# Splits, norm and queue order around the block turns of a three-product FFN phase

## The reference

```python
def conv_ffn(h, conv_hist, w_up, w_dw, b_dw, w_down):
    up = h @ w_up                                   # 1024 -> 2*2816
    ext = jnp.concatenate([conv_hist, up], axis=1)
    c = ext[:, 0:T] * w_dw[0] + ext[:, 1:T + 1] * w_dw[1] + ext[:, 2:T + 2] * w_dw[2] + b_dw
    a, b = jnp.split(c, 2, axis=-1)
    return (jax.nn.silu(a) * b) @ w_down, ext[:, -(CONV_W - 1):]
...
ffn, new_conv = conv_ffn(x1, conv_hist, w_up, w_dw, b_dw, w_down)
ple = jax.nn.sigmoid(x1 @ w_pg) * (pe @ w_pe)
x2 = layer_norm(ALPHA * x1 + ffn + ple, ln2_g, ln2_b)
```

## Time and profile before

| | |
|---|---|
| time, median of 3 runs | 3105.6 us (3100.81 to 3105.85) |
| profiled execution, own time | 3105.37 us |
| its span | 3103.6 us |
| busy in the span: PE, DVE, ACT, POOL | 92%, 68%, 47%, 41% |
| FFN phase in the span | 1444 to 3104 us |

### The profile page before, as it was taken

How to read it: one execution, slowest core, us unless ns; L and a number is a source line. 1 busy time by engine, 2 the same in 40 slices (tenths; PEclk the granted TensorE clock), 3 DMA queues, 4 the chain that set the end, 5 groups by cost and what they waited for, 6 DMA issues and landing times. The chain is left out here.

```text
span 3103.6 us, 47421 instructions
## 1 busy us (share of the span) xinstructions
PE 2870.4 (92%) x14597; PEld 2481.3 (80%) x14597; DVE 2119.3 (68%) x2977; ACT 1458.5 (47%) x2959; POOL 1265.7 (41%) x932
## 2 busy tenths in 40 slices
PE   8998998999998899998799999779999987899996
PEld 6877786777776788887788888768999986788885
DVE  5635677877776444445678777776787779677776
ACT  4333556777876222214335444433454454355553
POOL 5332645766766433334243333342222225222223
PEclk9997998999999999999999999899999998999998
DMA  4226451222233333325533232542333343333331
GB/s 134 85 81 138 147 162 41 56 51 43 42 90 125 111 101 101 109 99 181 163 101 110 95 132 101 163 137 87 112 105 97 102 158 117 114 115 118 113 106 53
DMA packets 234858, 333.26 MB, mean 107 GB/s; under 512 B 66896, under 2 KB 109616, under 8 KB 233360
## 3 DMA queue, kind: packets, MB, share of 16 engines
q1 hardware_dynamic: 234736, 331.76, 34.9%
HBM read 246.05 MB, written 85.63 MB: 107 GB/s over the span
## 5 line engine op out<-in xcount | busy, mean ns | idle before, releaser
L3059 DVE TENSOR_TENSOR mx_w_lo<-ff_w_raw,mx_w_hi 128x512 fp32r<-128x512 f32 x302 | 287.7, 957 | 14.3 <-ACT mx_w_hi L2873 14.3
L3116 DVE TENSOR_TENSOR ho_raw<-ho_raw,ff_d 128x512 f32<-128x512 f32 x264 | 169.3, 682 | 139.1 <-PE ff_d L86 117.9
L1567 POOL TENSOR_TENSOR at_p_lo<-at_p,at_p_hi 128x512 fp32r<-128x512 f32 (+2 forms) x160 | 188.7, 1180 | 162.9 <-ACT at_p_hi L1604 161.0
L2769 POOL TENSOR_TENSOR mx_odd<-ff_d_raw,mx_odd 128x512 fp32r<-128x512 f32 x66 | 101.5, 1537 | 375.9 <-ACT mx_odd L2882 375.7
L2873 ACT ACTIVATE mx_w_hi<-ff_w_raw 128x512 fp32r<-128x512 f32 x390 | 229.4, 622 | 31.9 <-POOL ff_w_raw L2757 29.6
L2882 ACT ACTIVATE mx_odd<-ff_d_raw 128x512 fp32r<-128x512 f32 x66 | 41.3, 626 | 418.9 <-PE ff_d L86 401.7
L1597 ACT ACTIVATE at_p<-at_s 128x512 f32<-128x512 f32 (+1 forms) x320 | 170.4, 533 | 109.2 <-PE at_s L1793 56.2
L1709 DVE TENSOR_TENSOR at_p_lo<-at_p,at_p_hi 128x512 fp32r<-128x512 f32 (+1 forms) x160 | 189.0, 1182 | 43.1 <-ACT at_p_hi L1604 42.2
L2733 POOL TENSOR_TENSOR mx_w_lo<-ff_w_raw,mx_w_hi 128x512 fp32r<-128x512 f32 x88 | 121.3, 1378 | 224.2 <-ACT mx_w_hi L2873 224.2
L3092 DVE SCALAR_TENSOR_TENSOR ff_cv_a<-ff_up_a,ff_taps,ff_cv_a 128x768 f32<-128x768 f32 (+1 forms) x132 | 163.3, 1237 | 61.1 <-ACT ff_cv_a L2939 33.3
L84 PE MATMUL ff_d<-mx_odd,ff_h_hi 128*128 128x512 f32 x364 | 148.7, 409 | 42.1 <-DVE ho_raw L3116 19.9
(11 more groups left out here) (556 smaller groups left out, 9980.9 us busy)
## 6 DMA issues: line engine op xcount, KB each, us to landing
ff_w_raw<-in_w_ffn_p SPq DMA_DIRECT2D x216, 256.0 KB, 3.3
ff_w_raw<-scratch_sums SPq DMA_DIRECT2D x176, 256.0 KB, 2.7
ff_d_raw<-in_w_ffn_p SPq DMA_DIRECT2D x132, 256.0 KB, 2.8
scratch_sums<-ff_w_raw SPq DMA_DIRECT2D x84, 256.0 KB, 3.7
ho_raw<-in_x SPq DMA_DIRECT2D x17, 512.0 KB, 4.3
mx_m_raw<-scratch_mix_t SPq DMA_DIRECT2D x17, 512.0 KB, 5.2
scratch_x_t<-mx_work SPq DMA_DIRECT2D x17, 512.0 KB, 2.6
scratch_y<-mx_work SPq DMA_DIRECT2D x17, 512.0 KB, 2.9
```

What stands on the lines that cost most here:

```text
L1567: pool.tensor_tensor(p_lo[:, e % H_RING, 0:b - a], p[:, e % P_RING, 0:b - a], f32(p_hi[:, e % H_RING, 0:b - a]), ALU.subtract).then_inc(lo ...
L2769: pool.tensor_tensor(lo, d_raw[:, :], f32(hi), ALU.subtract).then_inc(dlo, 1)
L3059: dve.tensor_tensor(w[j][1], raw, f32(w[j][0]), ALU.subtract).then_inc(wlo_dve, 1)
L3116: dve.tensor_tensor(y[t][:, H[i]], y[t][:, H[i]], ps_d[2 * (t % 2) + i][:, :], ALU.add)\
```

## The change

- Token lows T1 and T4 of blocks 1 and 2 are made on DVE instead of POOL. On ACT, T2's high moves from the end of a block to the beginning of the next.
- The norm of blocks 0 and 1 is two DVE instructions per tile (`normalise`: subtract mean and times gain; times 1/sigma and plus bias) and the power on POOL (`root`), in periods 0 and 1 of the next block, instead of four steps on three engines. The norm of block 2, at the end of the kernel, stays.
- ACT does copies 1 and 2 ahead of the down highs and of the weight and token highs that stood before them; down highs 1 and 3 move from ahead of `product_hi` to behind copy 1, down high 2 behind copy 2 and S2's high.
- DVE does `hidden_low` and join 0 right behind S4's low, ahead of the lows of A22, A11 and A12. In even periods S1's low stands ahead of the first add instead of behind it.
- SP issues the loads of y one by one through the periods: in block 0 through period 1, later through periods 1 and 2, each store of a tile ahead of its load.

The core of the diff:

```diff
-POOL_X = (T1, T4)
-DVE_X = (B11, B21, T2, T3, B22)
+POOL_X = ((T1, T4), (), ())
+DVE_X = tuple(tuple(j for j in range(PRODUCTS) if j not in POOL_X[b]) for b in range(3))
...
@@ SP
             def even_loads(b, f, p, at_next, at_d, turning=False):
+                if turning:
+                    load_y(b, 3)
+                    if BLOCKS[b] > 4:
+                        load_y(b, 4)
+                    for t in range(5, BLOCKS[b - 1]):
+                        store_y(b - 1, t)
+                    for t in range(5, BLOCKS[b]):
+                        load_y(b, t)
                 next_loads(b, f, p, 0, at_next, () if b == 0 else (A11, A22))
                 load_down(b, p, at_d, 0)
-                if turning:
-                    for t in (2, 3):
-                        load_y(b, t)
...
-                    if turning and j in (4, 5):
-                        for t in (2 * j - 8, 2 * j - 7):
-                            store_y(b - 1, t)
-                if turning:
-                    for t in (0, 1):
-                        load_y(b, t)
+                    if turning and b == 0 and j > 0:
+                        load_y(0, j - 1)
+                    if turning and b > 0 and 0 < j < 6:
+                        store_y(b - 1, j - 1)
+                        if j > 2:
+                            load_y(b, j - 3)
...
-                    for t in range(BLOCKS[0]):
-                        load_y(0, t)
-                odd_loads(b, 1, 0, 3, (-1, 12), turning=b > 0)
+                odd_loads(b, 1, 0, 3, (-1, 12), turning=True)
@@ POOL
+            def root(b, tiles):
+                for t in tiles:
+                    pool.wait_ge(eps, FIRST[b] + t + 1)
+                    pool.tensor_tensor(rstd[:, t:t + 1], var_eps[:, t:t + 1], power[:, :], ALU.pow).then_inc(rs, 1)
...
                     down_lows(b - 1, LAST, (3,))
-                    tokens(b, POOL_X)
-                    offsets(b - 1, range(BLOCKS[b - 1]))
-                    scale(b - 1, range(0, 4))
+                    root(b - 1, range(BLOCKS[b - 1]))
                     even(b, 0, 0)
-                    down_lows(b, 0, (1,))
-                    scale(b - 1, (4,))
-                    down_lows(b, 0, (2,))
-                    scale(b - 1, (5,))
-                    weight_low(b, 2, S3)
-                    weight_low(b, 2, S4)
+                    odd(b, 1, 0)
@@ ACT, period
+                if begins and b > 0:
+                    tokens(b, (T2,))
                 copy(b, f, i, 0)
...
-                if i == 1:
-                    down_highs(b, p, (0, 1) if at_end(b, p) else (1,))
-                elif before is not None:
-                    down_highs(before[0], before[2], (3,))
+                if at_end(b, p) and i == 1:
+                    down_highs(b, p, (0,))
                 if more:
                     weights(nb, nf, (A11,))
                 carry_in(b, f, p, i, 1)
                 if before is not None:
                     product_hi(*before[:4])
+                if begins and b > 0:
+                    tokens(b, (T3,))
+                copy(b, f, i, 1)
+                if i == 1:
+                    down_highs(b, p, (1,))
+                elif before is not None:
+                    down_highs(before[0], before[2], (3,))
                 if more:
                     weights(nb, nf, (A12,))
                 if begins:
-                    tokens(b, (T3, B22, T4) if b else (B22, T4))
-                copy(b, f, i, 1)
+                    tokens(b, (B22, T4))
                 if x_next:
                     tokens(b + 1, (B11,))
-                if centring is not None:
-                    centre(b - 1, centring[0])
-                if i == 1:
-                    down_highs(b, p, (2,))
                 copy(b, f, i, 2)
                 if more:
                     weights(nb, nf, (S2,))
+                if i == 1:
+                    down_highs(b, p, (2,))
@@ DVE
+            def normalise(b, tiles):
+                dve.wait_ge(ln_in, 32)
+                for t in tiles:
+                    n = FIRST[b] + t + 1
+                    dve.scalar_tensor_tensor(y[t], y[t], neg_mean[:, t:t + 1], ln_g[:, :], ALU.add, ALU.mult)\
+                       .then_inc(gained, 1)
+                    dve.wait_ge(rs, n)
+                    dve.wait_ge(gained, n)
+                    dve.scalar_tensor_tensor(y[t], y[t], rstd[:, t:t + 1], ln_b[:, :], ALU.mult, ALU.add)\
+                       .then_inc(shifted, 1)
...
                     convolve(*before, 0)
+                    if begins:
+                        tokens(b, (T2,))
                     convolve(*before, 1)
                     gate(*before)
-                    weights(b, f, (S4, A22), par)
...
+                    weights(b, f, (S4,), par)
+                    hidden_low(*before)
+                    join(b, f, par, 0)
+                    weights(b, f, (A22,), par)
+                    if begins:
+                        tokens(b, (T1,))
+                    weights(nb, nf, (A11, A12) if more else ())
...
+                        if t == 3:
+                            tokens(b, (T4,))
                 join(b, f, par, 1)
...
                 if more:
                     weights(nb, nf, (S2,))
+                if norm[1]:
+                    normalise(b - 1, norm[1])
                 if par == 0:
+                    weights(nb, nf, (S1,) if more else ())
                     if adds is not None and isinstance(adds[1], int) and adds[1] == 0:
                         dve.wait_ge(y_in, 16 * (FIRST[b] + BLOCKS[b]))
                     if adds is not None:
                         add(*adds, 0)
-                    weights(nb, nf, (S1,))
-                    if adds is not None:
                         add(*adds, 1)
...
-                period(b, 0, 0, (b - 1, FT - 1, LAST, 1) if b else None, after_last=b > 0)
+                period(b, 0, 0, (b - 1, FT - 1, LAST, 1) if b else None, after_last=b > 0,
+                       norm=((), (), (0, 1)) if b else none)
                 dve.wait_ge(const_in, 16)
-                period(b, 1, 1, (b, 0, 0, 0), shifts=((), (), (0, 1), (2, 3)) if b else none)
-                period(b, 2, 0, (b, 1, 0, 1), adds=(b, 0), shifts=((4,), (5,), (), ()) if b else none)
+                period(b, 1, 1, (b, 0, 0, 0), norm=((2,), (3,), (4, 5)) if b else none)
+                period(b, 2, 0, (b, 1, 0, 1), adds=(b, 0))
```

More of the change, by code:

```diff
@@ L2780, in offsets @@
                 for t in tiles:
[L2781 to L2784, removed]
+                    root(b, (t,))
+                    pool.wait_ge(rs, FIRST[b] + t + 1)
                     pool.tensor_tensor(offset[:, t:t + 1], neg_mean[:, t:t + 1], rstd[:, t:t + 1], ALU.mult)\
@@ L2789, in scale @@
                 for t in tiles:
[L2790 removed]
+                    pool.wait_ge(centred, t + 1)
                     pool.tensor_tensor(y[t], y[t], ln_g[:, :], ALU.mult).then_inc(scaled, 1)
@@ L2971, in centre, with period @@
                 for t in tiles:
-                    act.wait_ge(offs, FIRST[b] + t + 1)
+                    act.wait_ge(offs, t + 1)
                     act.activation(y[t], y[t], ACT.Identity, scale=rstd[:, t:t + 1],
                                    bias=offset[:, t:t + 1]).then_inc(centred, 1)
-            def period(b, f, p, i, before, x_next=False, centring=None):
+            def period(b, f, p, i, before, x_next=False):
                 nb, nf = following(b, f, 1)
@@ L3016, in period @@
                     weights(nb, nf, (S1, S3))
-                if x_next:
-                    tokens(b + 1, (T2,))
-                if centring is not None:
-                    centre(b - 1, centring[1])
                 if i == 0 and not at_end(b, p):
@@ L3025, in _ @@
             for b in range(3):
-                period(b, 0, 0, 0, (b - 1, FT - 1, LAST, 1, 1) if b else None, centring=((0, 1), (2, 3)) if b else None)
+                period(b, 0, 0, 0, (b - 1, FT - 1, LAST, 1, 1) if b else None)
                 act.wait_ge(const_in, 16)
-                period(b, 1, 0, 1, (b, 0, 0, 0, 0), centring=((4,), (5,)) if b else None)
+                period(b, 1, 0, 1, (b, 0, 0, 0, 0))
                 period(b, 2, 1, 0, (b, 1, 0, 1, 1))
@@ L3130, in shift @@
             def shift(b, t):
-                dve.wait_ge(scaled, FIRST[b] + t + 1)
+                dve.wait_ge(scaled, t + 1)
                 dve.tensor_tensor(y[t], y[t], ln_b[:, :], ALU.add).then_inc(shifted, 1)
-            def period(b, f, par, before, adds=None, x_next=False, after_last=False, shifts=((), (), (), ())):
-                def shift_tiles(n):
-                    for t in shifts[n]:
-                        shift(b - 1, t)
+            def normalise(b, tiles):
[8 more added lines that the diff above has]
+                       .then_inc(shifted, 1)
@@ L3140, in period @@
+            def period(b, f, par, before, adds=None, x_next=False, after_last=False, norm=((), (), ())):
```

(38 more changed lines are left out.)

15 lines of the change are left out of this document (4 added, 11 removed).

## The result

The changed kernel takes 3083.1 us (median of 4 runs, 3078.9 to 3087.4) against 3104.6 for the kernel before: ratio 0.9933, 95% interval 0.9915 to 0.9950. It is 21.5 us faster; 45.5 were forecast. The profiled execution took 3087.4 us, the longest of the four, with a span of 3085.5, 18.1 us less than that of the earlier trace rows.

What follows compares the result with a forecast made beforehand. PE, busy in 92% of the span, was taken as the bound, so only its pauses and lower clock could be won: 13 + 2 + 17 + 1 + 10 + 0 + 2.5 = 45.5 us, 3105.4 to 3060 us, range 3038 to 3088.

Steps and rivals of the forecast that it cites:

- these four terms: Gains forecast outside the pairs: start 13 us, turn to block 1 17, turn to block 2 10, end 2.5.
- a risk of the stores: Turns, rival: stores delay y loads 8 us, costing 8 us per turn, 3076; chance 0.22 shared with DVE as bound.
- The terms +2, +1 and 0: Gains forecast for the pairs: block 0 2 us, block 1 1 us, block 2 none.
- D2's charge: Block 0's pairs: D2 waits for the later add, charged 1.7 us per pair against 1.9 us won.
- have no cover to break that I can see: +1: Block 1's pairs: S1's low ahead of the add and later product_hi do no harm; gain 1 us, bounds −3 and +4.
- Net 0: Block 2's pairs: one high less ahead of copy 1, down high 2 ahead of `begin`; 0 us, bounds −5 and +5.
- VectorE becomes the bound in the turns: Turns, rival: DVE's added work delays gate and S4's low, copy 1 gains nothing; 3073 to 3080, chance 0.22 with late y loads.
- The other side: Block 0's pairs, rival: first add queued behind S1's low makes D2 wait 6 us per pair; 3105 to 3115, chance 0.06.
- The reorder frees the pairs as well: Pairs, rival: block 0 wins 12 to 16 us, block 2 up to 15; about 3035, chance 0.14.
- the 0.9 that was to show: Turns, sign that the forecast is right: granted clock at 0.9 or above.
- a sign against: Opening of a block, sign of being wrong: a new PE wait for tokens, as ACT makes T2's high there.

Runs made afterwards that it cites:

- the mix: Changed kernel with the first add ahead of S2's low in all blocks, and down highs 1 and 3 back ahead of product_hi in blocks 1 and 2 only: 3029.1 us.

## Why the prediction was wrong

**Start, turns and end: the sum was nearly right, two of its causes were not.** 42.5 us were forecast for these four terms, 39.9 came (11.4 + 17.7 + 9.8 + 1.0). The start's A22 wait and the turns' waits for the adds went, as forecast, and putting the y order back returned 33 us. In the start the prediction gave the copy's new place and the y loads together; the run with the y order back shows that the copy's place alone only moves the wait to another product. In the turn to block 1, S3 of periods 1 and 2 came 7.6 and 5.1 us earlier, where 7.7 and 6.6 were forecast, but POOL's scales were the smaller part of it: with the norm put back, S3 still came 5.8 and 3.8 us earlier than before the change. What brought those was not tried apart. The norm pays through the time at which y is stored and loaded again, a path that the prediction had listed only as a risk of the stores. That 17.7 us came in this turn where 17 were forecast is therefore in part luck.

The y loads were to land 4 us ahead of the first add. They do not; DVE still waits for the last of them in the turn to block 1:

```profile
DVE ho_raw L3110 <- DMA ff_y<-scratch_y: 1.0, 1, 1.0
```

In the turns, the new norm and the new order of the loads need each other. The two turns take 149.0 and 141.0 us with neither, 146.5 and 139.6 with the norm alone, 145.6 and 139.6 with the order alone, and 132.0 and 128.4 with both. In the start the order alone gives 9.8 us.

**The pairs: this is where it failed.** The terms +2, +1 and 0 were −1.8, −8.2 and −10.8. By the profiled executions the forecast missed by 27.4 us (45.5 − 18.1), and 23.8 of them are here.

*Block 0.* The stretch has nine pairs, not the ten of the sum. Both waits of 0.96 us went and D2's charge came, as argued; it was mis-sized, 2.4 us a pair where 1.7 was charged. S1's low is 0.7 of it, as charged (1.7 is left with S1's low late). The late down high 3 on the way to POOL's sums is about 0.7 too, where 1 was charged (1.7 is left with down highs 1 and 3 back). The remaining 1.0 us was in no term and was not tried apart; PE, no longer held by the two small waits, may simply come to the same add earlier. With the add ahead of the lows the block took 407.7 us, 25.6 less than before: the reorder frees the pairs if the add is not queued behind a sum of POOL.

*Blocks 1 and 2.* The failed step is "have no cover to break that I can see: +1" and, for block 2, "Net 0". The prediction counted the places of down highs 1 and 3, not what hangs on them: high 1, its low on POOL, the load into the one buffer, high 2. A high that comes later behind copy 1 makes high 2's data late, high 2 holds S1's and S3's highs and `begin`, POOL's two lows land on the convolution, and the next gate, product_hi and copy 1 are later. Put back, highs 1 and 3 alone gave 12 and 17 us, more than these blocks had lost. Counted from the first product of an even period of block 1 (means of seven), copy 1 starts at 8.59 us in the changed kernel and at 7.30 with highs 1 and 3 back. Of these 1.29 us, 0.71 are there when the convolution begins and 0.50 come in its first two steps, beside POOL; no run tries the two apart. S1's low ahead of the first add, the other half of the named step, cost 5 and 6 us as well. With the highs back, moving the add ahead of it gives only −0.2 and 1.6 us more, so in these blocks this cost is a part of the same lateness.

*Rivals.* "VectorE becomes the bound in the turns" gave nearly the measured time, but not for its reason: the turns came as forecast, and the loss was in the pairs. "The other side" had the right place in block 0 and would have needed 6.3 us a pair; 2.4 came. "The reorder frees the pairs as well" is what the mix does, not the change.

*Signs.* Norm steps were to take 1.36 us. In the turn to block 1, DVE's first and second norm step and the convolution:

```profile
L3133 DVE SCALAR_TENSOR_TENSOR ho_raw<-ho_raw,ff_neg_mean,ff_ln_g 128x1024 f32<-128x1024 f32 x4 | 7.2, 1788 | 0.0
...
L3137 DVE SCALAR_TENSOR_TENSOR ho_raw<-ho_raw,ff_rstd,ff_ln_b 128x1024 f32<-128x1024 f32 x4 | 5.1, 1284 | 0.4
...
L3086 DVE SCALAR_TENSOR_TENSOR ff_cv_b<-ff_up_b,ff_taps,ff_cv_b 128x768 f32<-128x768 f32 x8 | 8.7, 1088 | 0.5 <-ACT ff_cv_b L2933 0.4
```

The convolution is near its quiet 1.02 us, and of the norm only the first step is held up, so its two steps take 1.54 us on average. The clock in the turns, 0.88 and 0.87, stayed under the 0.9 that was to show: waits of about 5 us for copy 1 and for POOL's down low remain. The new wait for T2's low at the opening, named as a sign against, came with 3.6 us.

Two steps of the convolution took 3.86 us beside POOL's two lows, and with those lows on DVE the step in block 2 fell from 1.108 to 0.749 us. In the first case the four instructions together took 4.53 us from the first start to the last end, and alone they take 4.62 (two lows of 1.29 and 2.04 us for the two steps), so they ran as good as one after the other. The Trainium skill, "SBUF — State Buffer", section "Who interferes with whom", has an exclusive lock between a DVE instruction with two SBUF inputs and a GpSimd instruction that reads SBUF; the trace agrees.

POOL's low takes 1.29 us alone and DVE's 0.68, and moving 36 of them made block 2's pairs 13.6 us shorter, though DVE's busy time there grew from 269.4 to 282.3 us. The Trainium skill's "GPSIMD Engine Reference", section "4.1 Engine selection", sends elementwise work to VectorE; the runs agree.

## What to carry to other kernels

When a step is moved back on one engine, follow what it starts through a single buffer (low, next load, next high) before calling it free; a step with nothing behind it on its own engine can still head a chain over three others. Put what PE waits for ahead of work whose input is a longer chain, on an in-order engine above all. And where two edits meet at one wait, as norm and y order do, each alone shows little, so test them together and apart.

## What was not expected of the hardware

The first norm step (128x1024) took 1.27 us in some places and 2.29 in others of the same turn, the second 1.28 throughout: a mean of 1.79 is a mixture, not a price. The long ones are those that start while a low of POOL runs: one such low started at 2030.53 us, the step at 2030.85, and the step ended at 2033.14, about where 1.29 and 1.27 us one after the other would end. And in block 0's pairs DVE was busy 331.8 of 433.3 us before the change and 332.8 of 407.7 with the add first: the order in the queues, not an engine's load, was what cost time there.
